# A hybrid encoder layer in fp32: full rows from ScalarE and VectorE, residual rows loaded early and stored last, one attention chunk moved ahead of a turning

## What is computed

```
def encoder_layer(x, ...):
    h = rms_norm(x, norm_mix_pre)
    proj = h @ w_in                                  # 1024 x 4128
    attn = rms_norm(neighbourhood_attention(q, k, v, attn_rpb), attn_out_norm)
    ssd = ssd_mixer(z, xbc, dt_raw, ...)             # Mamba-2 scan, both directions, gated, normalised
    mix = jnp.concatenate([attn, ssd], axis=-1) @ w_out
    x = x + rms_norm(mix, norm_mix_post)
    h = rms_norm(x, norm_ffn_pre)
    gate = depthwise_conv(h @ w_gate, ffn_conv_w, ffn_conv_b)
    f = (jax.nn.gelu(gate, approximate=True) * (h @ w_up)) @ w_down
    return x + rms_norm(f, norm_ffn_post)
```

## Time and profile before

| | us |
|---|---|
| median of 3 runs | 2983.18 |
| lowest and highest | 2980.25, 2986.35 |
| the profiled execution | 2991.11 |
| its span, first to last instruction | 2989.3 |
| its mean granted TensorE clock | 0.985 of full speed |

### The profile page before, as it was taken

The page is one execution under the profiler, slowest core; times in us unless marked ns, Lnnn a source line. Parts: engine busy times, 40 slices in busy tenths (PEclk is TensorE's granted clock), DMA queues, the critical chain, the costliest instruction groups (busy, mean ns, idle before and its releaser), DMA issues.

```text
span 2989.3 us, 36770 instructions
## 1 busy us (share of the span) xinstructions
PE 2850.7 (95%) x12912; PEld 2249.7 (75%) x12912; DVE 2009.1 (67%) x3103; ACT 1304.1 (44%) x2562; POOL 637.2 (21%) x834
## 2 busy tenths in 40 slices
PE   7999999899899999999999999998998999999996
PEld 5878787568677778878778787865676788888885
DVE  3657745674778887776647567457757777777756
ACT  4325555356642333344533255553655333333443
POOL 4622222450214440000100322235402100000001
PEclk9999999899999999999999999999999999999998
DMA  7541233103624541153532422331146122214334
GB/s 220 139 146 55 65 110 102 67 27 125 223 87 168 193 172 51 64 175 117 190 102 71 127 62 70 117 127 27 64 129 202 63 84 85 71 50 150 100 116 138
DMA packets 143576, 332.75 MB, mean 111 GB/s; under 512 B 17746, under 2 KB 18418, under 8 KB 143393
## 3 DMA queue, kind: packets, MB, share of 16 engines
q1 hardware_dynamic: 106032, 200.42, 21.0%
q0 software_dynamic: 37360, 129.97, 13.3%
HBM read 264.49 MB, written 67.80 MB: 111 GB/s over the span
## 4 chain that ended last, share of the span: by engine, by line
PE 56%; DVE 7%; issue 3%; POOL 2%; ACT 2%; DMA 2%; DVEq 0%; ACTq 0%; SPq 0%; POOLq 0%
PE A L1066 4%; PE A L1068 4%; PE A L1067 4%; PE A L1118 4%; PE A L1120 4%; PE A L1119 4%; PE G L1066 4%; PE G L1068 4%; PE G L1067 4%; PE G L633 2%; PE G L635 2%; PE G L634 2%; DVE wlo L1695 1%; PE G L663 1%; PE G L665 1%
## 5 line engine op out<-in xcount | busy, mean ns | idle before, releaser
L1695 DVE TENSOR_TENSOR wlo<-raw,whi 128x512 fp32r<-128x512 f32 x630 | 447.7, 717 | 522.2 <-ACT whi L1194 519.8
L1194 ACT CAST whi<-raw 128x512 fp32r<-128x512 f32 x630 | 383.5, 619 | 493.4 <-PE A L1120 150.9
L633 PE MATMUL G<-arena_rounded,whi 128*128 128x512 f32 x800 | 332.1, 415 | 16.3 <-DVE wlo L1695 13.5
L634 PE MATMUL G<-arena_rounded,whi 128*128 128x512 f32 x800 | 317.3, 397 | 0.0
L635 PE MATMUL G<-arena_rounded,wlo 128*128 128x512 f32 x800 | 317.2, 397 | 0.0
L1066 PE MATMUL G<-arena_rounded,whi 128*128 128x512 f32 x560 | 222.3, 397 | 3.3 <-DVE small L2255 1.8
L1066 PE MATMUL A<-arena_rounded,whi 128*128 128x512 f32 x560 | 222.1, 397 | 2.0 <-DVE small L2255 1.1
L1068 PE MATMUL G<-arena_rounded,wlo 128*128 128x512 f32 x560 | 221.5, 396 | 0.0
L1068 PE MATMUL A<-arena_rounded,wlo 128*128 128x512 f32 x560 | 221.5, 396 | 0.0
L1067 PE MATMUL G<-arena_rounded,whi 128*128 128x512 f32 x560 | 221.5, 395 | 0.0
L1067 PE MATMUL A<-arena_rounded,whi 128*128 128x512 f32 x560 | 221.5, 395 | 0.0
(11 more groups left out here) (348 smaller groups left out, 6302.3 us busy)
## 6 DMA issues: line engine op xcount, KB each, us to landing
raw<-w_gu_tiles SPq DMA_DIRECT2D x184, 256.0 KB, 3.2
raw<-w_out_rows SPq DMA_DIRECT2D x144, 256.0 KB, 2.9
raw<-w_tok_tiles SPq DMA_DIRECT2D x96, 256.0 KB, 2.7
raw<-w_in_tiles SPq DMA_DIRECT2D x92, 256.0 KB, 2.8
raw<-sums_of_down SPq DMA_DIRECT2D x88, 256.0 KB, 2.7
raw<-w_down_rows SPq DMA_DIRECT2D x66, 256.0 KB, 2.7
f_by_chunk<-small POOLq DMA_DIRECT2D x24, 512.0 KB, 4.5
arena<-w_down_rows POOLq DMA_DIRECT2D x22, 512.0 KB, 7.2
```

The lines of the kernel that those rows point to most:

```text
L633: nc.tensor.matmul(out, whi[:, u % SPLIT_SLOTS, w], hi, start=first, stop=False)
L634: nc.tensor.matmul(out, whi[:, u % SPLIT_SLOTS, w], lo, start=False, stop=False)
L1194: nc.scalar.copy(whi[:, u % SPLIT_SLOTS, w], weights_of(u)).then_inc(S["hi_split"], 1)
L1695: tt(wlo[:, u % SPLIT_SLOTS, w], weights_of(u), whi[:, u % SPLIT_SLOTS, w].bitcast(F), ALU.subtract).then_inc(S["lo_split"], 1)
```

## The change

It does four things.

1. Full rows: ScalarE scales a turned bank into the full row (plain fp32). The high part of even banks is a ScalarE cast of it, that of odd banks a VectorE cast, and VectorE subtracts it from the full row. TensorE may reuse a bank once the full row is made. GpSimd adds nothing any more.
2. x: eight places instead of four (two more rows of the arena, two of `small`), all loaded at the start, the second four when the first have landed. The sums of rows 4 to 7 are stored first, those of rows 0 to 3 after them, with two waits for stores that have to land on the way; VectorE waits for the first of them ahead of bank 12 and for the second ahead of the first product.
3. In g = 0 the turnings stand before chunks 0, 2, 2 and 3 instead of 0, 1, 2 and 3.
4. VectorE makes the low part of piece 8 ahead of the gate's convolution instead of behind it.

```diff
                         if k >= 4:
-                            pe.wait_ge(S["norm_applied"], nth("norm_applied", N_FRONT + n - 3))
+                            pe.wait_ge(S["full_done"], nth("full_done", n - 3))
...
-                        if g == 0 and q < 4:
-                            turn_y(q)
+                        for c in {0: (0,), 2: (1, 2), 3: (3,)}.get(q, ()) if g == 0 else ():
+                            turn_y(c)
...
+        def x1_row(i):
+
+            return t(i - 1) if i >= 6 else arena[:, (K + i) if i < 4 else 14 + i - 4, :]
...
+                def turned_full(n):
+
+                    half, k = divmod(n, KD)
+                    act.wait_ge(S["xt_done"], nth("xt_done", N_FRONT + n + 1))
+                    nc.scalar.mul(full(k, half), turned_bank(n, "ffn_pre"), col("ffn_pre", k)).then_inc(S["full_done"], 1)
+                    if n % 2 == 0:
+                        act.wait_ge(S["full_done"], nth("full_done", n + 1))
+                        first_part(n, h_hi(k, half), full(k, half))
...
+                def rest_of_full(n):
+
+                    half, k = divmod(n, KD)
+                    if n % 2:
+                        dve.wait_ge(S["full_done"], nth("full_done", n + 1))
+                        after(nc.vector.tensor_copy(h_hi(k, half), full(k, half)))
+                    else:
+                        dve.wait_ge(S["hi_done"], nth("hi_done", N_FRONT + n // 2 + 1))
+                    tt(h_lo(k, half), full(k, half), h_hi(k, half).bitcast(F), ALU.subtract).then_inc(S["norm_applied"], 1)
...
                 for n in range(8, 16):
-                    turned_lo(n, "ffn_pre", N_FRONT)
+                    if n == 12:
+                        dve.wait_ge(S["x1_saved"], nth("x1_saved", 32))
+                    rest_of_full(n)
...
-                dve.wait_ge(S["full_done"], nth("full_done", 8))
+                dve.wait_ge(S["full_done"], nth("full_done", 16))
                 combined(1)
                 combined(3)
+                split_to(uend(j_gu(0)) + 3)
                 dve.wait_ge(S["gate_copied"], nth("gate_copied", 1))
                 gate_conv(0, range(3))
-                split_to(uend(j_gu(0)) + 3)
...
+                for i in range(4, TT):
+                    load_residual(i)
+                for n, i in enumerate((4, 5, 6, 7, 0, 1, 2, 3)):
                     pool.wait_ge(S["x1_ready"], nth("x1_ready", i + 1))
                     settled()
-                    pool.dma_start(x1_dram[i * P:(i + 1) * P, :], arena[:, K + i % 4, :]).then_inc(S["x1_saved"], 16)
...
+                    pool.dma_start(x1_dram[i * P:(i + 1) * P, :], x1_row(i)).then_inc(S["x1_saved"], 16)
+                    if n == 1:
+                        pool.wait_ge(S["x1_saved"], nth("x1_saved", 32))
+                    if n == 3:
+                        pool.wait_ge(S["x1_saved"], nth("x1_saved", 64))
```

More of the change, by code:

```diff
@@ L1507, in x1_stats @@
                     act.wait_ge(S["x1_ready"], nth("x1_ready", i + 1))
-                    after(nc.scalar.activation(unused, arena[:, K + i % 4, :], ACT.Square, accum_out=stat[:, 2, i:i + 1]))
+                    after(nc.scalar.activation(unused, x1_row(i), ACT.Square, accum_out=stat[:, 2, i:i + 1]))
                     nc.scalar.activation(stat[:, 2, i:i + 1], stat[:, 2, i:i + 1], ACT.Sqrt, bias=epsc[:, :], scale=1.0 / D
@@ L1538, in _ @@
                         n = 2 * (51, 52, 54, 55).index(v)
-                        turned_hi(n, "ffn_pre", N_FRONT)
-                        turned_hi(n + 1, "ffn_pre", N_FRONT)
+                        turned_full(n)
+                        turned_full(n + 1)
                 mix_stats(6)
@@ L2064, in hx_out @@
                     at = inverse(stat[:, 2, i:i + 1])
-                    ts(t(i % 4), arena[:, K + i % 4, :], at, None, ALU.mult).then_inc(S["hx_ready"], 1)
+                    ts(t(i % 4), x1_row(i), at, None, ALU.mult).then_inc(S["hx_ready"], 1)
                 y_lo(0)
@@ L2079, in _ @@
                         n = 2 * (52, 53, 55, 56).index(v)
-                        turned_lo(n, "ffn_pre", N_FRONT)
-                        turned_lo(n + 1, "ffn_pre", N_FRONT)
+                        rest_of_full(n)
+                        rest_of_full(n + 1)
                     if v in MIX_SCALED:
@@ L2140, in f_product @@
                         up = f_home(p)
+                    if p == 0:
+                        dve.wait_ge(S["x1_saved"], nth("x1_saved", 64))
                     tt(f_home(p), up, t(1), ALU.mult).then_inc(S["f_ready"], 1)
@@ L2557, in load_residual @@
                 def load_residual(i):
[L2559 to L2565, removed]
+                    pool.dma_start(x1_row(i), x[s, i * P:(i + 1) * P, :]).then_inc(S["x_res3" if i % 4 == 3 else f"x1_in{i % 4}"], 16)
                 pool.wait_ge(S["u_ready"], nth("u_ready", TT))
@@ L2572, in _ @@
                     load_residual(i)
-                for i in range(TT):
+                for i in range(4):
+                    if i < 3:
+                        pool.wait_ge(S[f"x1_in{i}"], 16 * (s * X1_LOADS[i] + 1))
+                    else:
+                        pool.wait_ge(S["x_res3"], 16 * (2 * s + 1))
+                settled()
+                for i in range(4, TT):
+                    load_residual(i)
+                for n, i in enumerate((4, 5, 6, 7, 0, 1, 2, 3)):
                     pool.wait_ge(S["x1_ready"], nth("x1_ready", i + 1))
                     settled()
-                    pool.dma_start(x1_dram[i * P:(i + 1) * P, :], arena[:, K + i % 4, :]).then_inc(S["x1_saved"], 16)
-                    if i < 4:
-                        pool.wait_ge(S["x1_saved"], nth("x1_saved", 16 * (i + 1)))
-                        pool.wait_ge(S["hx_ready"], nth("hx_ready", i + 1))
-                        settled()
-                        load_residual(i + 4)
-                    if i == 3:
-                        for n in range(4):
-                            full_rows(0, n)
-                for n in range(4):
-                    full_rows(1, n)
+                    pool.dma_start(x1_dram[i * P:(i + 1) * P, :], x1_row(i)).then_inc(S["x1_saved"], 16)
[3 more added lines that the diff above has]
+                        pool.wait_ge(S["x1_saved"], nth("x1_saved", 64))
                 pool.wait_ge(S["xt_done"], nth("xt_done", N_FRONT + N_FFN))
```

6 lines of the change are left out of this document (3 added, 3 removed).

## The result

| | before | after |
|---|---|---|
| median of 6 runs, us | 2985.23 | 2950.78 |
| lowest and highest | 2980.25, 2986.93 | 2943.52, 2962.25 |
| the profiled execution | 2991.11 | 2952.77 |
| its span | 2989.3 | 2951.0 |
| its granted TensorE clock | 0.985 | 0.989 |

The ratio is 0.9888 (0.9867 to 0.9909): the change saves 33 us (27 to 40). The direction was right, and so were three of the four places; one place gave nothing, and the size was too small.

A forecast was written before the change was run, and what follows sets the result against it. TensorE, busy 95% of the span, was taken as the bound, so only its idle or lower-clock time could be won. Terms of 12.3 and 12.1 us per sequence, together 24.4, gave 2958.8 us from 2983.18; range 2953 to 2970.

The forecast's parts named there:

- place 1: TensorE's 3.08 us wait before the second turning, for VectorE's last gated row; moving attention's second chunk wins 0.9 us per sequence.
- place 2: TensorE's waits before output chunks, 742 to 784 us; early x loads and late stores win 3.0 and 3.9 us.
- place 3: First half of the full rows, the 38 us after 784 us; without GpSimd's sums 2.3 us won per sequence.
- place 4: Full rows' second half, pads and piece 8, TensorE waits near 847 and 857 us; 4.9 and 3.4 us won.
- clock in place 4: Lower granted TensorE clock after the long waits there goes with them: 1.2 and 1.6 us won.
- the lead: TensorE's 0.9 us gain by the end of the fourth turning, claimed to be kept up to 740 us.
- rival (d): Better: waits of place 1 to place 4 vanish altogether, 34.0 us won, 2949 us; chance 0.06.
- the longer block of ScalarE: Full rows' first half: ScalarE's block between splits grows from 1.26 to 1.95 us, 0.7 us new wait per half.
- Rival (c): Slower: late stores delay GpSimd's clearing of the pads, holding pieces 6 and 7; 2992 us at 25 us landing; chance 0.03.
- The cover against late stores: At the pads: GpSimd's clearing can start at 838.2 us, ScalarE asks at 841.9 us, leaving 3.7 us.
- The rule of the Trainium skill: VectorE's casts within SBUF block GpSimd's DMA descriptors; four could push last stores and pads by up to 1.6 us.

The follow-up runs named there:

- the 54 waits: Changed kernel, with TensorE waiting for its own last matmul behind 54 pieces of the down projection, 27 per sequence: 2970.31 us, 0.9954 against the kernel before.
- the repeated run: The changed kernel run once more, unaltered, for a second profile: 2947.92 us, 0.9881 against the kernel before.

## Why the prediction was right in its direction and wrong in its size

The error in the four places, term by term, for both sequences together (us):

| | predicted | measured | what the difference is |
|---|---|---|---|
| place 1 | 1.8 | 0.00 | missed a condition |
| idle time, place 2 | 6.9 | 8.04 | new wait 0.3, not 0.9 |
| idle time, place 3 | 4.6 | 3.84 | one late load in sequence 2 |
| idle time, place 4 | 8.3 | 9.43 | new waits 0.4, not 1.0 |
| clock in place 4 | 2.8 | 2.79 | both dips gone, 1.25 and 1.54 |
| waits beyond their idle time | 0 | 5.82 | no such term |
| sum | 24.4 | 29.92 | |

The row of the clock is read from the starts of matmuls: in the dips of place 4 they are 0.427 us apart instead of 0.233, with 1.25 us lost behind piece 8 in sequence 1 and 1.54 us behind piece 6 in sequence 2.

**The term that was mis-sized: the waits.** Every term of the sum but the clock's was idle time before less idle time after, so what a wait costs beyond the idle time shown stood at nothing. The views list 29 waits in places 2 to 4 before, both sequences together, and 12 after. 29.9 us less the idle times and the clock leaves 5.8 us. 17 waits at 0.26 us, the price that the 54 waits gave at another place of the kernel, are 4.4 us of it. The other 1.4 us are matmuls that started late with no idle time listed, behind the listed waits: at 783.08, 792.62 and 798.80 us of the trace of before, and at the same matmuls in sequence 2. The 5.8 us are the whole difference to the forecast in these places, since the other rows of the table nearly cancel (-1.80 + 1.14 - 0.76 + 1.13 - 0.01 = -0.30).

**Place 1: the step that failed** is "From there to 740 us TensorE has no idle time ... so the lead is kept". Up to there the working held: the 3 us wait became waits of 0.27, 0.31, 0.41 and 0.31 us, and the chunk behind the fourth turning started 7.4 us after the first low part began instead of 8.4 us. But the lead was given back one chunk later. The fifth chunk, the first one that reads the turned rows, needs the fourth row's low part, which VectorE could not make sooner. In the trace of before a short wait stood there that it does not list: its first matmul starts 0.37 us after the last of the fourth chunk instead of 0.233, and no idle time is shown, since the matmul before is shown until 681.43 us. I had followed VectorE's chain to the low part of the second row (676.96 us), which the fourth turning needs, and not to that of the fourth row.

**Place 2** came by the cause that I gave it. The end of the working was too cautious: a scaling or a sum of VectorE between two pieces held TensorE once, by 0.33 us, not by 0.9 us. With the loads in time the splitting stays far enough ahead. In this place rival (d), which I had called unlikely, was nearer the truth. The total is near rival (d)'s 2949 us as well, but not by its way: it wanted place 1's waits and all the new ones gone, but place 1 gave nothing and 7.2 us of idle time are left in places 2 to 4, so the nearness is luck.

**Place 3** went as worked out in sequence 1: the low parts take 0.69 us again, the longer block of ScalarE costs 0.49 us (0.7 forecast), and the wait for a late load between stores that I had left standing is there, 0.76 us (0.69 in the earlier trace rows). In sequence 2 that load was later, ScalarE waited 2.1 us for it and TensorE 1.64. In the repeated run it was 0.56 us. That load is the one thing that still swings here.

**Place 4** went by the order that I had worked out. VectorE's timeline, at the low parts of pieces 6 and 7, at that of piece 8, and at the end of the convolution:

```profile
833.68 1.29 DVE L1709 TENSOR_TENSOR wlo<-raw,whi 128x512 fp32r<-128x512 f32 x2
...
839.43 0.69 DVE L1709 TENSOR_TENSOR wlo<-raw,whi 128x512 fp32r<-128x512 f32 x1
...
842.20 1.28 DVE L2156 SCALAR_TENSOR_TENSOR small<-small,prm 128x1024 f32<-128x1024 f32 x1
```

The changed kernel is 9.3 us ahead here (an earlier start of 0.86, and 4.88 and 3.58 won in places 2 and 3). With these added back, piece 6 is ready at 843.7 us, piece 8 at 849.4, and the convolution ends at 852.8; the forecast had 843.8, 849.6 and 853.0. The cast, and the wait at piece 10:

```profile
L1725 DVE CAST arena_rounded<-arena x16: 415/420/443, 784.1 to 2288.5; 128x512 fp32r<-128x512 f32 x16
...
852.77 0.47 PE L638 MATMUL G<-arena_rounded,whi 128*128 128x512 f32 x1 [0.42 <-DVE wlo L1709]
```

The cast takes 0.42 us, where I had 0.45 between bounds of 0.41 and 0.72. Such tenths of a microsecond decide the waits: piece 9 was in time (no wait instead of 0.2), piece 10 late by 0.42 instead of 0.8. The two waits of 0.58 us at 829.2 and 832.8 us of the trace of before, which the prediction left alone, are still there. The dips of the clock go with the long waits: of ten passages of place 4 in the kernels that keep a long wait at piece 6 or 8, nine show a dip, and of ten in the kernels that keep neither, none does. Where a dip falls decides what it costs. In sequence 2 of before it fell between pieces 6 and 8, and the wait at piece 8 was 1.80 us instead of the 3.33 of sequence 1: the 1.53 us less are what the dip had taken. Only the dip behind piece 8, in sequence 1, made the place longer (43.61 us against 42.30).

**Rival (c), the pads,** did not happen. The stores landed in 6.4 us at most, against the 20.5 that it needed. The cover against late stores was larger than the 3.7 us that I had worked out: from GpSimd's last store, 827.37 us, to ScalarE's cast at 832.47 us there are 5.1 us, since the clearing waited for TensorE's turning and not for a store. I made no run that delays the stores, so from which landing on it would decide is not shown. **The rule of the Trainium skill** (SBUF — State Buffer, "SBUF: two separate sides") would have had VectorE's casts keep GpSimd from writing its descriptors. GpSimd's stores took 0.53 or 0.54 us to issue throughout and landed in 4.1 us in the median against 4.6 before. A cast did fall among them: VectorE's cast at 826.13 us lies within the 2.10 us in which GpSimd issued the last four stores, and these followed one another as fast as without it. The cast took 0.44 us instead of 0.42. So the traces show no effect of that rule on the issues here; one cast lies so in each sequence of both traces of the changed kernel, and longer ones were not tried.

**What stays open.** The two profiled spans differ by 38.3 us. 29.9 lie in the four places and 8.4 elsewhere. Outside place 4 and up to its last matmul the trace of before was at the lower level for 20.4 us more than that of after. At the rate of place 4, where 6.8 us of dips cost 2.8 us, this makes 8.4 us, an estimate. Within one program the timed runs differ by as much, so it need not belong to the change. The timed gain, 33.4 us (27 to 40), and that of the repeated run, 35.5 (31 to 39), are 3 to 6 us above 29.9, which is inside the first interval and just outside the second. The median granted clock was 0.988 over the runs of before beside the repeated run and 0.990 in that run; whether the change itself leaves fewer dips outside place 4 stays open.

## What to carry to other kernels

Where TensorE is busy 95% of the time, weigh a wait by the distance between the starts of matmuls and not by the idle time that is shown: in places 2 to 4, 17 fewer waits and the short delays behind them were worth 5.8 us that no listed idle time shows, and a delay of 0.14 us showed none at all. When an edit moves work ahead of a wait, follow the engines that feed it past the point where the wait was, up to the next operation that needs their last product; if that product comes no earlier, reorder their work and not the waiting engine's. And when loads come late in a stretch, look first at what else was put on the DMA engines there.

## What the runs showed of the hardware

- A wait of TensorE between matmuls of 128 x 512 costs 0.26 us beyond the idle time shown, even if the awaited event is the end of its own last matmul (0.32 us in all, 54 waits).
- A VectorE cast of 128 x 512 within SBUF to rounded fp32 takes 0.42 us, ScalarE's 0.62 us. The subtraction beside it takes 0.69 us.
- The granted clock was at its lower level for 38 to 72 us per run up to the last matmul in ten traces, most of it outside the changed stretch, with matmuls 0.427 us apart instead of 0.233 (in place 4). Traces of kernels that run the same instructions there differ in it, and timed runs of one program differ by 11 us along with their granted clock (2991.4 at 0.985, 2980.5 at 0.989), so two spans should not be compared before that is taken out.
- A dip ahead of a long wait cost nothing here: 1.54 us of it in place 4 were made up by a wait 1.53 us shorter.
